# An encoder of two layers on one core: layers written out, the first layer's projections in passes over six PSUM banks, no preparation after the second layer

## What is computed

```python
x = layer_norm(x, ln0_g, ln0_b)
for i in range(DEPTH):                       # DEPTH = 2
    mix = hybrid_mixer(x, w_in[i], ...)      # h = x @ w_in; two kinds of attention of 8 heads; o @ w_out
    x = layer_norm(ALPHA * x + mix, ln1_g[i], ln1_b[i])
    ffn = conv_glu(x, w_up[i], conv_w[i], conv_b[i], w_down[i])
    gate = sigmoid(x @ w_ple_gate[i] + b_ple_gate[i])
    x = layer_norm(ALPHA * x + ffn + gate * (p[i] @ w_ple[i]), ln2_g[i], ln2_b[i])
```

## Time and profile before

| | us |
|---|---|
| median of 3 runs (1259.63 to 1260.17) | 1260.01 |
| the profiled execution, its own time | 1259.45 |
| its span, first to last instruction | 1257.6 |
| PE busy | 1223.7 |
| DVE, POOL, ACT busy | 570.7, 539.1, 486.8 |

### The profile page before, as it was taken

One profiled execution on the slowest core, in us unless ns is written; L12 is line 12 of the kernel. 1 busy time (PEld: TensorE's weight loads), 2 busy tenths in 40 slices (PEclk: granted clock), 3 DMA queues, 4 the chain that ended last, 5 costly groups with the idle time before them and its releaser, 6 DMA issues.

```text
span 1257.6 us, 17927 instructions
## 1 busy us (share of the span) xinstructions
PE 1223.7 (97%) x6152; PEld 1026.3 (82%) x6152; DVE 570.7 (45%) x864; ACT 486.8 (39%) x855; POOL 539.1 (43%) x276
## 2 busy tenths in 40 slices
PE   7999999999999999999999999999999999999996
PEld 6778888888888888888878888888888888888885
DVE  7887765842122224211498676575322122431117
ACT  3446553325433433233143665532443343332321
POOL 6532315446444444344274312334654444434433
PEclk9999999999999999999999999999999999999998
DMA  6321204234323332223132202314443333323331
GB/s 213 101 68 51 68 25 144 84 101 134 116 84 100 100 101 91 78 100 100 54 103 69 78 23 69 90 62 129 124 121 102 94 100 101 101 67 101 100 101 67
DMA packets 121317, 116.72 MB, mean 93 GB/s; under 512 B 4769, under 2 KB 95905, under 8 KB 121249
## 3 DMA queue, kind: packets, MB, share of 16 engines
q1 hardware_dynamic: 121248, 115.85, 29.9%
HBM read 113.74 MB, written 2.10 MB: 92 GB/s over the span
## 4 chain that ended last, share of the span: by engine, by line
issue 41%; POOL 27%; PE 22%; DVE 6%; DVEq 2%; POOLq 1%; DMA 1%; ACT 0%; SPq 0%; ACTq 0%
POOL w_lo L502 25%; PE ps L1189 4%; PE ps L1191 4%; PE ps L1190 4%; PE ps L1360 4%; PE ps L1346 2%; PE ps L1329 1%; POOL ln_r L508 1%; DVE hbuf L911 1%; PE ps L1331 1%; DVE stat L941 1%; PE ps L1371 1%; DMA x<-in_x_prompt_dram 1%; POOLq L501 1%; DVE row_max L949 1%
## 5 line engine op out<-in xcount | busy, mean ns | idle before, releaser
L502 POOL TENSOR_TENSOR w_lo<-raw,w_hi 128x1024 fp32r<-128x1024 f32 x192 | 467.2, 2437 | 540.2 <-ACT w_hi L590 540.2
L1189 PE MATMUL ps<-xt_hi,w_hi 128*128 128x512 f32 x704 | 273.9, 389 | 0.0
L1190 PE MATMUL ps<-xt_lo,w_hi 128*128 128x512 f32 x704 | 273.9, 389 | 0.0
L1191 PE MATMUL ps<-xt_hi,w_lo 128*128 128x512 f32 x704 | 273.9, 389 | 0.0
L590 ACT ACTIVATE w_hi<-raw 128x1024 fp32r<-128x1024 f32 x192 | 201.6, 1054 | 124.6 <-PE ps L1191 66.3
L1189 PE MATMUL ps<-w_hi,stat 128*128 128x512 f32 x480 | 190.0, 396 | 0.0
L1191 PE MATMUL ps<-w_hi,stat 128*128 128x512 f32 x480 | 187.2, 390 | 0.0
L1190 PE MATMUL ps<-w_lo,stat 128*128 128x512 f32 x480 | 187.1, 390 | 0.0
L1190 PEld LDWEIGHTS ps<-xt_lo,w_hi 128*128 128x128 f32 x704 | 132.2, 188 | 27.5
L1189 PEld LDWEIGHTS ps<-xt_hi,w_hi 128*128 128x128 f32 x704 | 132.2, 188 | 27.4
L1191 PEld LDWEIGHTS ps<-xt_hi,w_lo 128*128 128x128 f32 x704 | 132.2, 188 | 27.3
(11 more groups left out here) (120 smaller groups left out, 1392.7 us busy)
## 6 DMA issues: line engine op xcount, KB each, us to landing
raw<-in_w_up_dram SPq DMA_DIRECT2D x88, 512.0 KB, 3.8
raw<-in_w_down_dram SPq DMA_DIRECT2D x44, 512.0 KB, 3.3
raw<-in_w_in_dram SPq DMA_DIRECT2D x26, 512.0 KB, 3.7
raw<-in_w_out_dram SPq DMA_DIRECT2D x16, 512.0 KB, 3.8
raw<-in_w_ple_gate_dram SPq DMA_DIRECT2D x16, 512.0 KB, 3.9
scratch<-in_ln_g_dram SPq DMA_DIRECT2D x5, 512.0 KB, 4.6
scratch<-in_ln_b_dram SPq DMA_DIRECT2D x5, 512.0 KB, 6.2
raw<-in_w_ple_dram SPq DMA_DIRECT2D x4, 512.0 KB, 3.7
```

The costliest lines, as they stand in the source:

```text
L502: pool.tensor_tensor(w_lo[:, n, :], raw[:, n % RAW, :], w_hi[:, n, :].bitcast(F32), ALU.subtract).then_inc(w_split.sem, 1)
L1189: pe.matmul(out, a[0], b[0], start=first, stop=False)
L1190: pe.matmul(out, a[0], b[1], start=False, stop=False)
L1191: return pe.matmul(out, a[1], b[0], start=False, stop=last)
```

## The change

- Loops over the layers become written-out layers on every engine, so that the layers can differ; tables say at which group a transpose (`ROT_AT`) and a rotation (`ROTATE_AT`) stand, and which bank a projection uses (`WIN_BANK`, six banks).
- The first layer's tiles run by sequence: blocks 0 and 1 of tokens 0 and 1, then those of tokens 2 and 3. The first four are done in passes: all hi*hi (`hh`), then lo*hi (`lh`), then hi*lo (`hl`).
- Eight slots are loaded at the start rather than four, `w0` ahead of `ln0_b` and `x1`; the first normalisation's gain and bias have a buffer of their own; x3 is normalised inside layer 0.
- In both layers part of the rotations move behind the first scores. The second half of tile 7 stands at group 0, `win_part` 0 to 3 at groups 2 and 3, then one per group up to 15. Probabilities of groups 0 to 7 are all evacuated by ACT.
- The preparation of a third layer is dropped on SP, ACT, POOL, PE and DVE.

```diff
-WARM = (8, 9)
+WARM = (9, 1)
...
+FIRST = 8
...
+WINS = (((0, 0), (0, 1), (1, 0), (1, 1), (0, 2), (0, 3), (1, 2), (1, 3)),
+        ((0, 0), (0, 1), (0, 2), (0, 3), (1, 0), (1, 1), (1, 2), (1, 3)))
+WINS = tuple(w + tuple((2, t) for t in range(TT)) for w in WINS)
+WIN_BANK = (0, 1, 6, 7, 2, 3, 0, 1, 0, 1, 0, 1)
+ROT_AT = ({4: 1, 5: 2, 6: 4, 7: 6, 8: 8, 9: 10, 10: 13, 11: 17},
+          {6: 2, 7: 3, 8: 5, 9: 9, 10: 13, 11: 17})
+ROTATE_AT = ({5: 0, 6: 2, 7: 3, 8: 6, 9: 8, 10: 11, 11: 15},
+             {6: 0, 7: 2, 8: 4, 9: 7, 10: 11, 11: 15})
...
+def pe_plan(layer):
+
+    if layer == 0:
+        steps = [("hh", 0), ("lh", 0), ("hl", 0, 0), ("norm_in", 1), ("hh", 1), ("lh", 1), ("hl", 0, 1), ("hl", 1, 0),
+                 ("hl", 1, 1), ("norm_in", 2), ("hh", 2), ("lh", 2), ("hh", 3), ("lh", 3), ("hl", 2, 0), ("hl", 2, 1),
+                 ("hl", 3, 0), ("hl", 3, 1), ("norm_in", 3)]
+        for n in (4, 5, 6):
+            steps += [("win", n, 0), ("rot", n - 4), ("win", n, 1)]
+        steps.append(("rot", 3))
+    else:
+        steps = [("win", 0, 0), ("win", 0, 1), ("norm_in", 2), ("win", 1, 0), ("win", 1, 1), ("norm_in", 3)]
+        for n in range(2, 7):
+            steps += [("win", n, 0), ("rot", n - 2), ("win", n, 1)]
+        steps.append(("rot", 5))
+    steps.append(("win", 7, 0))
     for g in range(GROUPS + 3):
         if g < GROUPS:
             steps.append(("scores", g))
-            if g < 2:
-                steps += [("win_part", 2 * g), ("win_part", 2 * g + 1)]
-            elif g < 14:
-                steps.append(("win_part", g + 2))
+            if g == 0:
+                steps.append(("win", 7, 1))
+            elif g in (2, 3):
+                steps += [("win_part", 2 * g - 4), ("win_part", 2 * g - 3)]
+            elif 4 <= g < 16:
+                steps.append(("win_part", g))
...
-        if g == 1:
-            steps.append(("rot", 1, 3))
-        if g in (5, 9, 13, 17):
-            steps.append(("rot", 2, (g - 5) // 4))
+        steps += [("rot", n) for n in at_group(ROT_AT[layer], g)]
...
+            load_x(0)
+            sp.dma_start(first_g, bcast(ln0_g)).then_inc(first_gain_landed.sem, 16)
             first_load(0)
+            sp.dma_start(first_b, bcast(ln0_b)).then_inc(norm_landed.sem, 16)
+            load_x(1)
             first_load(1)
             first_load(2)
             load_x(2)
             first_load(3)
+            sp.dma_start(rope_sb[:, :, :, :], rope).then_inc(fixed_landed.sem, 16)
+            load_consts(0)
+            first_load(4)
+            first_load(5)
             load_x(3)
-            sp.dma_start(rope_sb[:, :, :, :], rope).then_inc(fixed_landed.sem, 16)
-
-            with sp.Fori(0, DEPTH) as layer:
+            first_load(6)
+            first_load(7)
+
+            for layer in range(DEPTH):
...
-                following = (layer + 1) % DEPTH
-                for s in range(AHEAD):
-                    raw_free(STREAM + s)
-                    load(s, source(s, following), 2)
+                if layer < DEPTH - 1:
+                    for s in range(AHEAD):
+                        raw_free(STREAM + s)
+                        load(s, source(s, layer + 1), 2)
...
             ln_root(0, 1)
+            first_lo(0)
             ln_root(1, 2)
-            first_lo(0)
             first_lo(1)
+            first_lo(2)
             ln_root(2, 3)
-            first_lo(2)
             first_lo(3)
+            first_lo(4)
+            first_lo(5)
             ln_root(3, 4)
-
-            with pool.Fori(0, DEPTH) as layer:
+            first_lo(6)
+            first_lo(7)
+
+            for layer in range(DEPTH):
...
+                for n, (c, t) in enumerate(WINS[layer][:2 * TT]):
+                    w = (HEADS, KV)[c]
+                    if layer and c == 0:
+                        body_lo(4 + n)
+                    pool.wait_ge(qk_ss.sem, qk_ss.at(layer, n + 1))
+                    pool.tensor_tensor(rqk[:, c, t, 0:w], rqk[:, c, t, 0:w], half_neg[:, 0:w],
+                                       ALU.pow).then_inc(qk_rstd.sem, 1)
+                    if layer and c == 1 or n >= 4:
...
+                if layer == 0:
+                    first_hi(3)
+                    norm_in(1)
+                    first_hi(4)
+                    first_hi(5)
+                    win(0)
+                    win(1)
+                    first_hi(6)
+                    norm_in(2)
+                    first_hi(7)
+                    win(2)
+                    win(3)
+                    norm_in(3)
+                    qkt_evac(0)
+                    win(4)
+                    qkt_evac(1)
+                    win(5)
+                    body_hi(8)
+                    body_hi(9)
+                    qkt_evac(2)
+                    win(6)
+                    qkt_evac(3)
+                    body_hi(10)
+                else:
+                    body_hi(4)
+                    win(0)
+                    norm_in(2)
+                    body_hi(5)
+                    win(1)
+                    norm_in(3)
+                    for n in range(2, 7):
                         body_hi(4 + n)
-                        if n == 2:
-                            qkt_evac(0, 0)
-                        win(c, t)
-                        if n < 2:
-                            norm_hi(n + 2, tr_full.at(layer, TR["norm_in", n + 2] + 1))
-                        else:
-                            qkt_evac(*divmod(n - 1, TT))
+                        qkt_evac(n - 2)
+                        win(n)
+                    qkt_evac(5)
                 for g in range(GROUPS + 3):
 
-                    if g == 2:
-                        qkt_evac(1, 3)
-                    if g in (6, 10, 14, 18):
-                        qkt_evac(2, (g - 6) // 4)
+                    for n in at_group(ROT_AT[layer], g - 1):
+                        qkt_evac(n)
                     if g in (15, 16, 23, 24, 31, 32):
                         heads_hi((g - 15) // 16, (g - 15) // 8 % 2, (g - 15) % 8)
-                    if g in (3, 7, 11, 15):
-                        win(2, (g - 3) // 4)
+                    if g == 1:
+                        win(7)
+                        body_hi(11)
+                    if g in (4, 8, 12, 16):
+                        win(8 + (g - 4) // 4)
...
+                if layer == 0:
+                    rotate(0)
+                    norm_lo(2, xt_hi_done.at(layer, 1))
+                    dve.wait_ge(x_landed[TT - 1].sem, 16)
+                    norm_stats(TT - 1)
+                    norm_centre(TT - 1, first_g)
+                    norm_scale(TT - 1, TT, first_b)
+                    rotate(1)
+                    norm_lo(3, xt_hi_done.at(layer, 3))
+                    qkt_lo(0)
+                    rotate(2)
+                    qkt_lo(1)
+                    rotate(3)
+                    qkt_lo(2)
+                    rotate(4)
+                    qkt_lo(3)
+                else:
+                    norm_lo(2, xt_hi_done.at(layer, 1))
+                    rotate(0)
+                    norm_lo(3, xt_hi_done.at(layer, 3))
+                    rotate(1)
+                    for n in range(2, 6):
+                        qkt_lo(n - 2)
+                        rotate(n)
+                    qkt_lo(4)
+                    qkt_lo(5)
                 for g in range(GROUPS + 3):
                     if g < GROUPS:
                         maxima(g)
-                    if g == 2:
-                        qkt_lo(1, 3)
-                    if g in (6, 10, 14, 18):
-                        qkt_lo(2, (g - 6) // 4)
+                    for n in at_group(ROT_AT[layer], g - 1):
+                        qkt_lo(n)
...
+                for step in STEPS[layer]:
                     kind = step[0]
-                    if kind == "win":
-                        _, c, t, half = step
+                    if kind == "hh":
+                        win_bank(step[1])
+                        win_pass(step[1], 0, 0, range(4), True, False)
+                    elif kind == "lh":
+                        win_pass(step[1], 1, 0, range(4), False, False)
+                    elif kind == "hl":
+                        _, n, half = step
+                        ins = win_pass(n, 0, 1, (2 * half, 2 * half + 1), False, True)
+                        if half:
+                            ins.then_inc(win_full.sem, 1)
...
+                def win_bank(n):
+
+                    earlier = [m for m in range(n) if WIN_BANK[m] == WIN_BANK[n]]
+                    if earlier:
+                        pe.wait_ge(win_free.sem, win_free.at(layer, earlier[-1] + 1))
+                    else:
+                        t = [b // 2 * 2 for b in DOWN_BANK].index(WIN_BANK[n] // 2 * 2)
+                        pe.wait_ge(down_free.sem, down_free.at(layer, t - 3))
+
+                def win_pass(n, a, b, quarters, first, last):
+
+                    c, t = WINS[layer][n]
+                    for q in quarters:
```

(23 more changed lines are left out.)

252 lines of the change are left out of this document (118 added, 134 removed).

## The result

The changed kernel takes 1278.04 us (median of 4 runs, 1276.60 to 1278.88), the one before 1259.82 in the same comparison: a ratio of 1.0141, 95% interval 1.0126 to 1.0156. It is slower by 18.2 us where 14.7 was forecast. The profiled execution took 1278.65 us, its span 1276.9.

A forecast was written before the change was run, and what follows sets the result against it. TensorE, busy 1223.7 of 1257.6 us, was taken as the bound. Terms 0.0 + 19.6 + 2.0 - 1.7 - 1.0 - 4.1 = +14.8 on 1259.45, plus 0.56, gave 1274.8, forecast as 1274.5; range 1261.5 to 1280.

The forecast's parts named there:

- startup, without clock: Start of layer 0: first product 4.1 us sooner and old waits gone, offset by new waits; sum 0.0 us.
- ring of layer 0, net: Layer 0's attention: TensorE's fillers wait on weight slots through five queues; 21.2 us of waits less old ones, +19.6.
- part 0, part 3, group 8: TensorE's waits in layer 0 ahead of filler parts 0 and 3 and at group 8: 9.45, 7.45, 0.65 us.
- clock: TensorE's granted clock falls after three long new waits: two fifths of 3 x 1.7, +2.0 us, bounds 0 and +5.
- layer 1 and fillers: Layer 1 loses old waits, -1.7 us; fillers at groups 14 and 15 cover half of the heads' waits, -1.0.
- tail: End of the kernel without a third layer's preparation: -4.1 us, bounds -1.6 and -5.0.
- Part 0's chain: Layer 0, end of scores 0 to filler part 0, through maxima, rotations, low half, load and exponentials: 17.0 us with hand-overs.
- second turn of the ring: Layer 0, part 0 to part 3, through lo(10), load(12), rotate(7) and lo(11): 13.0 us, TensorE filling 5.5, waiting 7.45.
- the +5 end: Upper bound for the clock: each of the three long waits pays for a lower clock behind it, +5 us.
- The startup did not run ahead: Rival: lo(7) ready before about 37 us, startup waits and up to 12 us gone; 1262.5, some 1260; chance 0.15.
- The ring was not hidden: Rival: layer 0's loads come early enough that rotations 5 to 7 hide behind fillers; 1253.5 us, chance 0.10.
- The third rival: Every long wait also halves the clock and meets more subtractions: +24 and +5, 1281.9, say 1280; chance 0.11.

The follow-up runs named there:

- The run with extra products: Changed kernel plus 160 and 110 small TensorE products into an unused bank ahead of filler parts 0 and 3 of layer 0: 1274.38 us.
- the best kernel: Changed kernel with layer 0's rotations, low halves, fourth root, x3's normalisation, angle tables, lo(0) and transposes moved: 1253.69 us, 0.9953 of the kernel before.

## Why the prediction was right, and where it was off

**Direction and cause: right.** The forecast was 1274.5 in a range of 1261.5 to 1280; 1278.04 was measured. The waits that it named stand where it put them. Terms against what the trace of the changed kernel shows (the clock's is an estimate, worked out below):

| term | predicted | measured |
|---|---|---|
| startup, without clock | 0.0 | +0.5 |
| of it: waits for lo(6), lo(7) | 4.0, 2.8 | 3.3, 2.5 |
| ring of layer 0, net | +19.6 | +19.4 |
| of it: scores 0, 1, 2 | 0.95, 0.4, 2.35 | 1.0, 0.5, 2.2 |
| of it: part 0, part 3, group 8 | 9.45, 7.45, 0.65 | 9.6, 6.8, 0.9 |
| clock | +2.0 | +7.2 |
| layer 1 and fillers | -2.7 | -3.7 |
| tail | -4.1 | -4.2 |

The waits are gaps between starts of PE's products, less a product's own 0.23 us. The startup's number is the first product 3.0 sooner and 3.7 of old waits gone, against 5.8 for the two low halves and three small waits, 0.5, 0.6 and 0.3, by the waits view. The terms add up to the 19.2 between the two profiled executions (1278.65 and 1259.45), but single ones are good to about 1 us only: the transposes of tile 1, 1.03 us long and now behind the first product, are in none of them, and the prediction left them out as well.

Part 0's chain (16.1 us from rows, 17.0 with hand-overs) came to 16.5, from the end of scores 0 at 75.11 to part 0 at 91.56. Part 3's wait is near its forecast, but not by the way that the prediction walked: its second turn of the ring goes through load(12), and in the trace that load kept nobody waiting, while PE's products and transposes behind part 0 did. So the size of this wait is in part luck.

**The clock was mis-sized.** That is the step that was off: "I take two fifths of 3 x 1.7", with no reason given for the two fifths. Three stretches of 5.4, 5.9 and 4.7 us have a granted clock of 0.50, 0.57 and 0.57; the share that is missing of each gives an estimate of 2.7, 2.5 and 2.0 us, 7.2 together. That is beyond even the bound of 5: every long wait (the two of the startup, 3.3 and 2.5 us, lie close together and share one stretch) was followed by such a stretch, and each was longer than the one of the earlier trace rows from which the price came, 3.40 us. The run with extra products shows that it is a cost of its own: 3.7 us for two of the three, where the estimate has 4.5. The third, in the startup, was not run by itself.

The Trainium skill (TensorE: Matmul & The Clock Gate, "Why this matters for your kernels") asks for no long idle gaps between bursts. The trace agrees for the three waits, and the +5 end, at which each of them pays, was nearer than the choice.

**Fillers and layer 1.** The fillers at groups 14 and 15 cover more of the waits for heads in layer 0 than the 0.5 us I took: in the kernel before PE waits 1.1, 0.8 and 0.4 us between 87 and 146 us, and all three are gone. Layer 1 gave 1.5 us by its landmarks, most of it ahead of its first product and at the gate. Its attention gave nothing: 0.1 between the first product and the output projection. Most of the old waits there did go, and a new one came that the prediction had not, PE waiting for the low halves of tile 6. Waits of PE in layer 1 of the changed kernel, 640 to 740 us, and two rows of DVE:

```profile
PE ps L1457 <- DVE stat L1039: 2.4, 1, 2.4
PE ps L1300 <- POOL w_lo L563: 1.1, 1, 1.1
...
715.08 2.26 DVE L1008 TENSOR_TENSOR hbuf<-scratch 128x256 f32<-128x256 f32 x1
717.27 2.47 DVE L1009 TENSOR_TENSOR scratch<-scratch 128x128 f32<-128x128 f32 x1
```

Rotation 7 meets two subtractions in a row there. The prediction knew the mechanism and used it for the startup alone.

**The startup's offset.** The first product came at 14.87, not 13.7. The first scale, which waits for its bias, was locked out by lo(0) (2.67 us at 9.57 instead of 1.28), and the transposes behind it ran at half clock (1.97 us instead of 1.09 in the best kernel). The scores of group 0 at 74.40 are 2.4 us behind the walk; the clock's stretch at 46.8, 2.7 by the estimate, is enough for that.

**The rivals.** The startup did not run ahead, for the reason given against that rival: the fourth root. That it would bring 12 us was too much in any case; with the root moved, the kernel gained 2.8, since DVE's list was late just behind it. The ring was not hidden. The third rival, longer waits with half clock after each, was right in its second half: its waits were no longer, its clock was.

## What to carry to other kernels

When steps are spread out to fill gaps, follow each of them through all queues to the load that it releases: a rotation moved two groups back held a `pow`, that a subtraction, that a load, that an exponential, and a filler at the end. Price every new idle time of TensorE twice, once for itself and once for the slow products behind it. And when taking away one wait gains less than the wait was long, read which engine the next wait is on: here it was DVE in most cases. Moving only what PE waited for brought 12.7 us with the rotations, and nothing more in the startup; the best kernel moved what POOL locked out as well, and which of its moves brought how much is open.
